# A decoder-step kernel on one core: the order of the matmuls inside a weight slot, by token half

## The reference: what is computed

```python
h = rmsnorm(x, norm1_g)
proj = h @ w_in                       # a1, a2, z, xbc, dt, u, v
y_a = silu(layernorm(causal_dwconv(a1 * sigmoid(a2)))) @ conf_w_out
y_b = rmsnorm(ssd(...) * silu(z)) @ ssm_w_out
y_c = (gelu(u) * chunk_spatial(layernorm(gelu(v)))) @ gmlp_w_out
gates = sigmoid(h @ w_gate + b_gate)  # three gates, one per branch
x = x + (gates0 * y_a + gates1 * y_b + gates2 * y_c) @ w_o
up = rmsnorm(x, norm2_g) @ ffn_w_up   # ag, av, 2816 channels each
x = x + (silu(causal_dwconv(ag)) * av) @ ffn_w_down
y = rmsnorm(x, final_norm_g)
```

## Time and profile before

| | us |
|---|---|
| median of three runs | 1003.36 |
| the profiled execution, its own time | 1004.03 |
| its span, first to last instruction | 1001.8 |
| PE busy | 984.0 |
| DVE busy | 607.3 |
| ACT busy | 437.6 |
| POOL busy | 310.8 |

### The profile page before, as it was taken

The page is one execution under the profiler, slowest core; times in us unless marked ns, Lnnn a source line. Parts: engine busy times, 40 slices in busy tenths (PEclk is TensorE's granted clock), DMA queues, the critical chain, the costliest instruction groups (busy, mean ns, idle before and its releaser), DMA issues.

```text
span 1001.8 us, 19136 instructions
## 1 busy us (share of the span) xinstructions
PE 984.0 (98%) x7849; PEld 963.6 (96%) x7849; DVE 607.3 (61%) x955; ACT 437.6 (44%) x619; POOL 310.8 (31%) x261
## 2 busy tenths in 40 slices
PE   8899999999999999999999999999999999999997
PEld 8799999999998999899999999999999999999997
DVE  7599799962645675797744247555540036565456
ACT  7554579575734775525233344444321132232120
POOL 0111111111111114344342444444433464444341
PEclk9899999999999999999999999999999999999999
DMA  7888769667765768315272223222223332321222
GB/s 227 251 184 181 164 144 151 143 128 169 160 149 125 181 143 223 110 64 168 85 257 84 85 85 105 85 84 84 63 63 95 115 106 86 93 79 52 70 71 90
DMA packets 52590, 125.24 MB, mean 125 GB/s; under 512 B 15920, under 2 KB 18864, under 8 KB 52528
## 3 DMA queue, kind: packets, MB, share of 16 engines
q1 hardware_dynamic: 43744, 97.09, 32.1%
q0 software_dynamic: 8640, 27.27, 15.5%
q10 hardware_dynamic: 144, 0.00, 0.0%
HBM read 116.41 MB, written 7.93 MB: 124 GB/s over the span
## 4 chain that ended last, share of the span: by engine, by line
PE 90%; DVE 3%; DMA 2%; SPq 2%; ACT 1%; issue 1%; DVEq 0%; ACTq 0%
PE accs L418 82%; PE accs L1438 2%; DMA w_split<-in_w_in_main 1%; DMA w_split<-in_w_gate 1%; PE misc L1213 1%; SPq L513 1%; DVE part L494 1%; PE misc L1178 1%; DMA w_raw<-in_w_in_main 1%; PE misc L1037 1%; PE misc L1218 1%; PE misc L1197 1%; DVE xbc L1945 0%; PE misc L1163 0%; PE misc L1229 0%
## 5 line engine op out<-in xcount | busy, mean ns | idle before, releaser
L418 PE MATMUL accs<-h_split,w_split 128*128 128x272 f32 x4608 | 584.4, 288 | 0.1
L418 PEld LDWEIGHTS accs<-h_split,w_split 128*128 128x128 f32 x4608 | 576.9, 188 | 5.6 <-issue 4.4
L418 PE MATMUL accs<-branch,w_split 128*128 128x272 f32 x2472 | 320.5, 290 | 7.0 <-DMA w_split<-in_w_in_main 5.0
L418 PEld LDWEIGHTS accs<-branch,w_split 128*128 128x128 f32 x2472 | 314.3, 189 | 11.7 <-DMA w_split<-in_w_in_main 5.2
L358 POOL TENSOR_TENSOR w_split<-w_raw,w_split 128x1024 fp32r<-128x1024 f32 (+2 forms) x104 | 234.7, 2264 | 209.5 <-ACT w_split L353 186.0
L353 ACT ACTIVATE w_split<-w_raw 128x1024 fp32r<-128x1024 f32 (+3 forms) x166 | 157.8, 959 | 202.0 <-PE accs L418 201.8
L1522 DVE SCALAR_TENSOR_TENSOR ca<-part,params,ca 128x512 f32<-128x512 f32 x120 | 82.5, 744 | 0.1
L366 POOL DMA_DIRECT2D w_split<-in_w_in_main x24 | 21.1, 879 | 153.7 <-ACT w_split L353 153.7
L2202 DVE TENSOR_TENSOR xbc<-accs,xbc 128x544 f32<-128x544 f32 x14 | 10.1, 725 | 87.7 <-PE accs L418 87.7
L352 ACT ACTIVATE w_split<-w_raw 128x1024 fp32r<-128x1024 f32 (+1 forms) x60 | 56.1, 936 | 15.9 <-PE accs L418 12.7
L2179 DVE TENSOR_TENSOR temps<-temps,mixed 128x512 f32<-128x512 f32 x22 | 40.7, 1850 | 26.5 <-ACT temps L1011 26.5
(11 more groups left out here) (280 smaller groups left out, 793.4 us busy)
## 6 DMA issues: line engine op xcount, KB each, us to landing
w_raw<-in_ffn_w_up SPq DMA_DIRECT2D x44, 512.0 KB, 3.6
w_raw<-in_w_in_main SPq DMA_DIRECT2D x28, 512.0 KB, 4.6
w_split<-in_w_in_main POOLq DMA_DIRECT2D x24, 512.0 KB, 8.0
w_raw<-in_w_gate SPq DMA_DIRECT2D x24, 512.0 KB, 3.9
w_split<-in_w_gate POOLq DMA_DIRECT2D x16, 512.0 KB, 7.9
w_raw<-in_ffn_w_down SPq DMA_DIRECT2D x16, 384.0 KB, 3.1
w_raw<-in_ffn_w_down SPq DMA_DIRECT2D x16, 320.0 KB, 2.9
xbc<-in_x SPq DMA_DIRECT2D x16, 272.0 KB, 5.8
```

What stands on the lines that cost most here:

```text
L418: mm = pe.matmul(accs[:, a, half, 0:HALF], w_split[:, s, wp, k * P:(k + 1) * P], rhs(s, k, xp, half), start=(first and k == 0 and n == 0), ...
```

## The change

In `pe_quad`, for quads without `ready`, the loop over the two token halves goes outside the loop over the pieces: all pieces of the left half (24 matmuls in a slot of eight pieces, 18, 15 or 12 in slots of six, five or four) add into the left bank, then the same into the right bank. Quads with `ready` keep the order of before, and so does the last quad of D2, which is written apart. The number of matmuls, of weight loads, their operands, the waits at the slot's start and the semaphore at its end stay.

```diff
-                for k in range(p.kb[s]):
-                    if ready is not None:
+                steps = [(half, k) for half in range(2) for k in range(p.kb[s])]
+                if ready is not None:
+                    steps = [(half, k) for k in range(p.kb[s]) for half in range(2)]
+                for half, k in steps:
+                    if ready is not None and half == 0:
                         ready(s, k)
-                    for half in range(2):
-                        for n, (wp, xp) in enumerate(((0, 0), (0, 1), (1, 0))):
-                            mm = pe.matmul(accs[:, a, half, 0:HALF], w_split[:, s, wp, k * P:(k + 1) * P],
-                                           rhs(s, k, xp, half), start=(first and k == 0 and n == 0),
-                                           stop=(last and k == p.kb[s] - 1 and n == 2))
+                    for n, (wp, xp) in enumerate(((0, 0), (0, 1), (1, 0))):
+                        mm = pe.matmul(accs[:, a, half, 0:HALF], w_split[:, s, wp, k * P:(k + 1) * P],
+                                       rhs(s, k, xp, half), start=(first and k == 0 and n == 0),
+                                       stop=(last and k == p.kb[s] - 1 and n == 2))
```

## The result

The changed kernel takes 1007.39 us (median of 20 runs) against 1004.19 us of the kernel before (20 runs now; the three that the prediction had gave 1003.36). The ratio of the runs is 1.0028, with a 95% interval of 1.0018 to 1.0038. That is 1.8 to 3.8 us slower, about 2.8 (the two medians lie 3.2 apart): clear of the measurement's spread, and within the 0.5% that the prediction called the same.

What follows compares the result with a forecast made beforehand. It took PE's nearly unbroken matmul stream as the bound. The bank term gave +0.8 us and all others 0, so 1003.36 became 1004.2 us on the median, with a range of 1000.0 to 1007.5.

Steps and rivals of the forecast that it cites:

- What bounds the kernel: Whole kernel: PE streams matmuls nearly without a hole, so only the start-to-start distance can move much; no accumulator waits.
- The bank, +0.8 us: All 5568 matmuls: fewer bank changes, priced at +0.15 ns each from L1438 against D2, +0.8 us, rounding 0.0 to +1.6.
- The order of the weights, 0: Weight loads within a bank: each group of three goes to the next piece, no load saved or added, 0.
- The order of the moving operand: Operand reads step from piece to piece; taken as 0, bounded for `h_split` by 0.82 ns per matmul, 3.2 us either side.
- The trial in the last quad: D2's last quad, L1438: first 75 `branch` matmuls, taken as already running the new order, 125.41 against D2's 125.26 ns.
- Waits and signals: Slot starts and ends: waits at the first matmul, signals at the last, releases when they were, 0.
- first use of operands: Quads whose operands are still being written keep the old order, so no wait piece by piece is stretched, 0.
- the slower rival: All slots, U2 first: steps within one bank wait for one another; 1007.4 us at `branch` rate, 1034 at bound; chance 0.18.
- Its own signs for the forecast: Profile after: U2's 960 matmuls at 119.5 to 119.9 us, D1 and D2 within 0.2 ns of 125.3, no accumulator waits.
- The rule on the banks: PSUM banks: by the skill page's rule of using all eight, one bank at a time should be slower, the slower rival's time.

Runs made afterwards that it cites:

- the run of the three orders: Kernel before, U1/U2 quads in all eight old/new combinations of bank, weight and operand order: 24.05 to 24.07 us with old operand order, 24.18 to 24.22 with new.
- the thirty orders: Kernel before, with only the order of the six matmuls of a piece changed, slot by slot in U1 and U2: 6.13 to 6.25 us per 48 matmuls.

## Why the prediction was right, and where it was off

The time lies in the range, 0.1 us below its upper end, and the step from before is within the 0.5% that the text called the same. The forecast's own step of +0.8 us was too small, and it was put on the wrong term: the sum had the bank at +0.8 and the order of the operand at 0, and the runs show 0 for the bank by itself, while the loss of some 2.9 us comes with the order of the operand (taken apart in U1 and U2, which hold 1.54 of it). The range held because the bound on that second term was kept at both ends, not because the sum was right. Point by point:

- *What bounds the kernel.* Right: nearly all of the 2.89 us is in the distance from matmul to matmul, and no wait of PE for accumulators appeared.
- *The bank, +0.8 us.* The separated orders give 0.00 us a quad for the bank by itself, so the 0.15 ns that were carried to all 5568 matmuls are not the bank's, and D2 in the new order didn't show them (125.18 ns). The trial in the last quad could not carry them either. Its 75 matmuls, untouched by the change, took 9.57 us before, 9.60 after and 9.62 in the run of the three orders, (9.62 - 0.29) / 74 = 126.1 ns against 125.41: the row differs from one execution to the next by more than was read from it. And L1438 doesn't run the order of the change: the two slots of a block follow each other in one half, so 30 matmuls in a row go to one bank, not 15, and the order of the operand's starts is another one too.
- *The order of the weights, 0.* Right, 0.00 us by itself.
- *The order of the moving operand, taken as 0 with 3.2 us to either side.* This is the term that was mis-sized. The reason given for the 0, that each matmul keeps its own operands and only its neighbours change, fails: the price hangs on the neighbours. U1 and U2 rose nearly by the bound itself, 1.54 us in their two rows together, 0.80 ns for each of their 1920 moved matmuls. Over the whole of `h_split` the busy time grew by 2.2 us, so the other 2016 moved ones, in VU, X, Z and the G phases, rose by some 0.3 ns each. D1's row adds 0.20 us; what is left lies in the phases ahead of U1. That `branch` against `h_split` in the same order gave a bound of the right size is in part luck: it is a difference of addresses, but the runs show no reason why a new order should cost just that.
- *Waits and signals, first use of operands, 0.* Right.
- *The rivals, and the signs.* The prediction said that U2 at 120.4 us would speak for the slower rival, and U2 took 120.40. Its own signs for the forecast failed, U2 at 119.5 to 119.9 and D1 within 0.2 ns of 125.3 (it took 125.62). The rival's price, `h_split` at the rate of `branch`, is nearly what U2 shows (125.24 against 125.26 ns). Its mechanism, that steps within one bank wait for one another, is refuted: new banks alone take 24.05 us a quad like the old ones. The right price came with a wrong cause. The measured 1007.4 us is the rival's figure by chance, since before's median of 20 runs is 0.8 us above the one that the rival started from.
- *The rule on the banks.* The Trainium skill's page "Perfetto Trace Analysis", section "Matmul Optimizations", asks to use all eight PSUM banks. Here 24 matmuls in a row into one bank cost as much as a change after every third, 24.05 us a quad both ways.

What stays open: why the slots of `h_split` ahead of U1 rose less than those of U1 and U2, by what rule neighbouring starts add up, and why `branch` and `h_split` at the same distance of 224 bytes differ.

## What to carry to other kernels

Where PE streams without a hole, reordering matmuls that are equal in shape can still move it, by some 2% among the thirty orders here, through the addresses that it reads, and the bank that it writes may have no part in it by itself. Whether a new order gains or loses hung on where the operand lay, so an order has to be tried at the addresses of the kernel at hand. Compare streams that differ in one thing only: a stretch that already runs something like the new order is a trial of just those parts of the change that it shares, and its row has to be steady from one execution to the next before a tenth of a nanosecond is read from it. And when one profiled execution is faster and the median slower, split the span at a point behind the unsteady start and compare the two pieces.

## What the runs showed of the hardware

- Where all matmuls of a quad read one operand start, the time from one 272-column matmul to the next hung on the distance between that start and the start of the weights in SBUF, within 256 bytes: 123.4 ns at 160 and 192 bytes, 126.6 to 126.7 at 64, 128 and 224, at the full granted clock (1.00). Moving both by 64 bytes changed nothing, moving either one did.
- The Trainium skill's page "TensorE: Matmul & The Clock Gate", section "Part 2: What happens when you issue a matmul", says that PE has two independent read ports, and that loading the next weights takes no read bandwidth from the running matmul. The measurement doesn't fit that: the price of as many matmuls and weight loads of the same shape went from 125.3 to 123.4 ns when only the weights' start was moved. What in the chip the two reads share, if anything, no run shows.
- A mix of starts is not the mean of its parts: `h_split` in the order of before takes 124.4 ns where the mean of its four starts, weighted by use, is 125.65, and thirty orders of the same six matmuls spread over 2.6 ns.
- Two tensors with the same distances in the same order agreed at one distance, 124.43 and 124.44 ns at 0 within 256 bytes, and differed at another, 125.5 and 126.7 ns at 224.
- The bank by itself cost nothing: 192 matmuls took 24.05 us with a change of bank after every third and with one in 24.
